# Expert queries computed from the unnormalised input, and the first expert choice made alone

## What is computed

```python
h2 = rms_norm(x, norm2_g) * (1.0 + scale2) + shift2
q = (h2 @ w_query).reshape(T, 8, 256)
s1 = einsum('thd,nd->thn', q[..., :128], sub_keys1)
s2 = einsum('thd,nd->thn', q[..., 128:], sub_keys2)
v1, i1 = top_k(s1, 16); v2, i2 = top_k(s2, 16)
top_s, top_p = top_k(v1[..., :, None] + v2[..., None, :], 16)
e_idx = i1[top_p // 16] * 128 + i2[top_p % 16]
gate = softmax(top_s)
act = gelu(einsum('cd,ced->ce', h2, expert_u[e_idx]))
x = x + gate2 * einsum('ce,ced->cd', gate * act, expert_v[e_idx])
```

## Time and profile before

| | us |
|---|---|
| median of three runs | 2176.35 |
| the three runs | 2176.57, 2171.0, 2176.35 |
| the profiled execution | 2177.08 |
| its span, first to last instruction | 2175.2 |
| PE busy, share of span | 1868.7, 86% |
| DVE busy | 1485.5, 68% |
| ScalarE (ACT) busy | 1016.9, 47% |
| POOL busy | 437.7, 20% |
| mean granted TensorE clock | 0.940 |
| retrieval stage, first gather issued | 433.14 |
| last gather issued | 1074.2 |

### The profile page before, as it was taken

How to read it: one execution, slowest core, us unless ns; L and a number is a source line. 1 busy time by engine, 2 the same in 40 slices (tenths; PEclk the granted TensorE clock), 3 DMA queues, 4 the chain that set the end, 5 groups by cost and what they waited for, 6 DMA issues and landing times. The chain is left out here.

```text
span 2175.2 us, 33251 instructions
## 1 busy us (share of the span) xinstructions
PE 1868.7 (86%) x12082; PEld 1393.0 (64%) x12082; DVE 1485.5 (68%) x2609; ACT 1016.9 (47%) x2046; POOL 437.7 (20%) x457
## 2 busy tenths in 40 slices
PE   4974897878888778777799989889999999779998
PEld 4842887644432222222279988678998988668997
DVE  6675554777767667666466675766677787676666
ACT  2444212445544444444355554467665545335554
POOL 0010220045454434434200000002231330210000
PEclk8987998889999999999999999699999999889999
DMA  8861001399999999999955655035555655224553
GB/s 327 292 219 34 3 3 41 109 406 420 419 419 420 419 420 419 420 420 420 386 185 184 192 172 202 1 116 176 191 181 177 192 175 174 93 84 160 186 189 98
DMA packets 104385, 497.31 MB, mean 229 GB/s; under 512 B 11856, under 2 KB 17232, under 8 KB 71376
## 3 DMA queue, kind: packets, MB, share of 16 engines
q1 hardware_dynamic: 66064, 225.41, 31.2%
q0 software_dynamic: 36864, 268.45, 29.8%
q10 hardware_dynamic: 1344, 1.96, 0.3%
HBM read 494.73 MB, written 1.05 MB: 228 GB/s over the span
## 5 line engine op out<-in xcount | busy, mean ns | idle before, releaser
L247 PE MATMUL ps<-srcs,wh 128*128 128x512 f32 x2064 | 743.2, 402 | 32.1 <-DVE srcs L261 20.4
L1874 PE MATMUL ps<-row,diag 128*128 128x512 f32 x1024 | 502.3, 626 | 121.4 <-ACT diag L1957 121.2
L249 PE MATMUL ps<-srcs,wl 128*128 128x256 f32 x2064 | 583.5, 283 | 0.0
L229 DVE TENSOR_TENSOR wl<-ring,wh 128x1024 fp32r<-128x1024 f32 x362 | 452.3, 1252 | 123.0 <-ACT wh L223 121.8
L247 PEld LDWEIGHTS ps<-srcs,wh 128*128 128x128 f32 x2064 | 392.5, 190 | 127.7 <-issue 35.9
L1874 PEld LDWEIGHTS ps<-row,diag 128*128 128x128 f32 x1024 | 184.0, 195 | 430.1 <-ACT diag L1957 271.7
L2050 DVE CUSTOM_DVE_ANT_0 row<-row,h_tok 128x1024 f32<-128x1024 f32 x256 | 313.8, 1226 | 198.6 <-DMA row<-in_peer_uv,experts 190.7
L223 ACT ACTIVATE wh<-ring 128x1024 fp32r<-128x1024 f32 x362 | 379.1, 1052 | 66.3 <-PE ps L249 43.5
L249 PEld LDWEIGHTS ps<-srcs,wl 128*128 128x128 f32 x2064 | 396.3, 192 | 2.0 <-issue 1.9
L1811 POOL DMA_INDIRECT row<-in_peer_uv,experts x256 | 281.5, 1100 | 393.1 <-PE ps L1874 342.9
L1950 ACT ACTIVATE acts<-dots 128x1 f32<-128x1 f32 x256 | 51.8, 202 | 329.4 <-DVE dots L2050 328.9
(11 more groups left out here) (503 smaller groups left out, 2083.0 us busy)
## 6 DMA issues: line engine op xcount, KB each, us to landing
ring<-in_stream SPq DMA_DIRECT2D x378, 512.0 KB, 3.7
alpha<-in_ada_late SPq DMA_DIRECT2D x12, 512.0 KB, 5.1
beta<-in_ada_late SPq DMA_DIRECT2D x10, 512.0 KB, 6.0
kappa<-in_ada_late SPq DMA_DIRECT2D x10, 512.0 KB, 5.9
row<-in_peer_uv,experts POOLq DMA_INDIRECT x256, 15.4
bias<-in_attn_bias SPq DMA_DIRECT2D x8, 256.0 KB, 5.0
w<-in_cmp_w SPq DMA_DIRECT2D x1, 2048.0 KB, 7.5
xT<-in_xT SPq DMA_DIRECT2D x1, 1024.0 KB, 15.9
```

The costliest lines, as they stand in the source:

```text
L229: nc.vector.tensor_tensor(wl[:, n % PAIRS, :], ring[:, tile % RING, :], wh[:, n % PAIRS, :].bitcast(F32), ALU.subtract).then_inc(tiles_fre ...
L247: nc.tensor.matmul(out, wh[:, n, cols], source.rearrange("p a t -> p (a t)"), start=start, stop=stop, skip_group_check=True)
L249: return nc.tensor.matmul(out[:, 0:S], wl[:, n, cols], source[:, 0, :], start=False, stop=stop, skip_group_check=True)
L1874: last = nc.tensor.matmul(y_part(t, half), diag[:, s % DIAGS, :], row[:, s % ROWS, D + half * 512:D + (half + 1) * 512], start=(slot == 0) ...
```

## The change

The query projection of (x g r + b) is split by linearity, where g is the gain, r the token's inverse root and b the shift.

For the first four query tiles (`UNSHIFTED` = 4) the matmuls take x g alone, split straight from `xT`, so they need neither the root nor the shift. The shift's part is a constant for each query channel: `constants()` multiplies the tile by `shifts` (b in two parts, two columns), 16 narrow matmuls for each tile. The evacuation `out(i)` then takes three DVE instructions: a reduce of the two columns, the sum of both product parts, and plus the constant times the *root* (not its inverse). What comes out is the query times the root. ScalarE multiplies the scores by the inverse root of the token when it copies them (`rstd_tok`, found by turning the root on PE and a reciprocal on 128x2). Tile 3 has its constants after its products, the others ahead of them.

`hT` becomes x g plus b times the root (eight ScalarE instructions, eight DVE instructions), again with the inverse applied on ScalarE's copy to `h_tok`. From it a *second split* (`second_high`, `second_low`) is made for tiles 4 to 15, after the first choice.

The sum of squares is cut (`sums_only`): six of the eight blocks are summed at the end of the projection, and the last two on PE at the start of the retrieval stage (`sum_squares`). `take_rstd` and the root are gone from the projection.

The order changes too. `choose(0)` has nothing among its steps. After it come tiles 2 and 3, `hT`, the gates of head 0, and the second low parts. `choose(1)` moves into the slots of head 0, ahead of `choose(2)`, with a dot before every fourth step in this head (every second in the others). Query tiles 4 and 5 come before the slots on PE, tiles 6 and 7 and scores 2 and 3 among the slots of head 0; from head 1 on, the tiles of head h + 3 lie among the slots of head h. `gate_exp(1)` stands at slot 8, and `finish_gates(1)` after slot 10.

The core of the diff (twelve blanks of indentation removed; the new names of semaphores and buffers, and `project`'s parameter, left out):

```diff
tile(i)
-        if stats:
+        if sums_only:
+            sum_squares(pe, squared, 0, KT - 2)
+        elif stats:
             mean_square(pe, squared, summed)
...
 first = take(T_QUERY)
-EARLY = 4
+EARLY, UNSHIFTED = 2, 4
+def ahead_of(head):
+    return head + 3 if head else NH
...
     return ps[:, 6 + h % 2, :]
+def const_columns(i):
+    return score_bank(min(i, 1))[:, i % 2 * 2:i % 2 * 2 + 2]
+root_bank = ps[:, 3, 0:S]
...
     def query(i):
+        n = split_no(first + i) % PAIRS
         pe.wait_ge(tiles_freed, first + i + 1)
...
             pe.wait_ge(query_out, i - 1)
+        def constants():
+            if i == 0:
+                pe.wait_ge(shift_low, 1)
+            if i % 2 and i > 1:
+                pe.wait_ge(const_out, i)
+            for k in range(KT):
+                cols = slice(k * P, (k + 1) * P)
+                nc.tensor.matmul(const_columns(i), wh[:, n, cols], shifts[:, k, :], start=(k == 0),
+                                 stop=False, skip_group_check=True)
+                last = nc.tensor.matmul(const_columns(i), wl[:, n, cols], shifts[:, k, :], start=False,
+                                        stop=(k == KT - 1), skip_group_check=True)
+            return last
+        if i < UNSHIFTED - 1:
+            constants()
         for k in range(KT):
...
                 pe.wait_ge(src_low, k + 1)
+            if i == UNSHIFTED:
+                pe.wait_ge(second_low, k + 1)
             last = product_both(query_bank(i), first + i, k, srcs[:, k], k == 0, k == KT - 1)
+        if i == UNSHIFTED - 1:
+            last = constants()
         last.then_inc(tiles_used, 1)
...
+    sum_squares(pe, None, KT - 2, KT).then_inc(summed, 1)
     query(0)
+    pe.wait_ge(root, 1)
+    for t in range(TT):
+        last = nc.tensor.transpose(root_bank[:, t * P:(t + 1) * P], rstd[:, t * P:(t + 1) * P], mat("ident"))
+    last.then_inc(root_turned, 1)
     query(1)
...
     score(0)
+    query(2)
+    query(3)
+    score(1)
     turn_h()
-    for h in range(1, EARLY):
-        query(2 * h)
-        query(2 * h + 1)
-        if h >= 2:
-            score(h - 1)
-    score(EARLY - 1)
+    query(4)
+    query(5)
...
         last.then_inc(v_used, 1)
-        ahead = s // TOPK + EARLY
+        ahead = ahead_of(s // TOPK)
+        if s == 1:
+            score(2)
+        if s == 4:
+            query(6)
+        if s == 8:
+            query(7)
+        if s == 13:
+            score(3)
         if ahead < NH:
...
             nc.scalar.activation(scores[t][:, :, h, :], score_bank(h)[:, 2 * t * NE:2 * (t + 1) * NE]
-                                 .rearrange("p (s n) -> p s n", s=2), ACT.Copy).then_inc(score_copied, 1)
+                                 .rearrange("p (s n) -> p s n", s=2), ACT.Copy,
+                                 scale=rstd_tok[:, t:t + 1]).then_inc(score_copied, 1)
...
+    nc.scalar.activation(shifts[:, :, 0], mod[:, 24:32], ACT.Copy).then_inc(shift_high, 1)
+    for k in range(KT):
+        nc.scalar.activation(srch[:, k, :], xT[:, k, :], ACT.Copy, scale=gs[:, 1, k:k + 1]
+                             ).then_inc(src_high, 1)
+    act.wait_ge(scaled, 1)
+    nc.scalar.activation(rstd[:, :], rstd[:, :], ACT.Sqrt).then_inc(root, 1)
+    weight_and_copy(0)
+    weight_and_copy(1)
+    high(act, first + AHEAD + 2)
+    act.wait_ge(inverted, 1)
+    copy_scores(0)
+    for k in range(KT):
+        nc.scalar.activation(hT[:, k, :], rstd[:, :], ACT.Copy, scale=mod[:, 24 + k:25 + k]
+                             ).then_inc(shifted, 1)
+    copy_low(2)
+    weight_and_copy(3)
+    gate_exp(0)
+    copy_scores(1)
+    act.wait_ge(tiles_used, split_no(first + UNSHIFTED - 1) + 1)
     for k in range(KT):
         act.wait_ge(normed, k + 1)
-        nc.scalar.activation(srch[:, k, :], hT[:, k, :], ACT.Copy).then_inc(src_high, 1)
-    weight_and_copy(0)
-    weight_and_copy(1)
-    copy_scores(0)
+        nc.scalar.activation(srch[:, k, :], hT[:, k, :], ACT.Copy).then_inc(second_high, 1)
     for t in range(TT):
...
         nc.scalar.activation(h_tok[:, t, :], ps[:, 2 * t:2 * t + 2, :].rearrange("p b n -> p (b n)"),
-                             ACT.Copy).then_inc(h_copied, 1)
-    for h in range(1, EARLY):
-        weight_and_copy(2 * h)
-        weight_and_copy(2 * h + 1)
-        if h >= 2:
-            copy_scores(h - 1)
-    copy_scores(EARLY - 1)
-    for head in range(LOOKAHEAD):
-        gate_exp(head)
+                             ACT.Copy, scale=rstd_tok[:, t:t + 1]).then_inc(h_copied, 1)
+    weight_and_copy(4)
+    weight_and_copy(5)
     for s in range(TT * SLOTS):
...
             act.wait_ge(gates_done, head + 1)
+        if s == 8:
+            gate_exp(1)
         act.wait_ge(dotted, s + 1)
...
                              ).then_inc(diag_ready, 1)
-        ahead = s // TOPK + EARLY
+        ahead = ahead_of(s // TOPK)
+        if s == 3:
+            copy_scores(2)
+        if s == 7:
+            weight_and_copy(6)
+        if s == 11:
+            weight_and_copy(7)
+        if s == 15:
+            copy_scores(3)
         if ahead < NH:
...
         dve.wait_ge(src_high, k + 1)
-        nc.vector.tensor_tensor(srcl[:, k, :], hT[:, k, :], srch[:, k, :].bitcast(F32), ALU.subtract
-                                ).then_inc(src_low, 1)
+        nc.vector.scalar_tensor_tensor(srcl[:, k, :], xT[:, k, :], gs[:, 1, k:k + 1],
+                                       srch[:, k, :].bitcast(F32), ALU.mult, ALU.subtract
+                                       ).then_inc(src_low, 1)
...
         dve.wait_ge(low_copied, i + 1)
-        if i >= 4:
+        if i >= UNSHIFTED:
             dve.wait_ge(scored, i // 2 - 1)
-        nc.vector.tensor_tensor(queries[:, i % 4, :], query_bank(i)[:, 0:S], low_part[:, i % 2, :], ALU.add
-                                ).then_inc(query_out, 1)
-    for k in range(KT + 2):
-        if k < KT:
-            nc.vector.scalar_tensor_tensor(hT[:, k, :], xT[:, k, :], gs[:, 1, k:k + 1], rstd[:, :],
-                                           ALU.mult, ALU.mult).then_inc(shifting, 1)
-            dve.wait_ge(shifting, k + 1)
-            nc.vector.tensor_scalar(hT[:, k, :], hT[:, k, :], mod[:, 24 + k:25 + k], None, ALU.add
-                                    ).then_inc(normed, 1)
-        if k >= 2:
-            low_of(k - 2)
+            nc.vector.tensor_tensor(queries[:, i % 4, :], query_bank(i)[:, 0:S], low_part[:, i % 2, :], ALU.add
+                                    ).then_inc(query_out, 1)
+            return
+        nc.vector.tensor_reduce(const[:, i % 2:i % 2 + 1], const_columns(i), AXX, ALU.add
+                                ).then_inc(const_out, 1)
+        nc.vector.tensor_tensor(whole[:, i % 2, :], query_bank(i)[:, 0:S], low_part[:, i % 2, :], ALU.add
+                                ).then_inc(whole_out, 1)
+        dve.wait_ge(const_out, i + 1)
+        dve.wait_ge(whole_out, i + 1)
+        dve.wait_ge(root, 1)
+        nc.vector.scalar_tensor_tensor(queries[:, i % 4, :], rstd[:, :], const[:, i % 2:i % 2 + 1],
+                                       whole[:, i % 2, :], ALU.mult, ALU.add).then_inc(query_out, 1)
+    dve.wait_ge(shift_high, 1)
+    nc.vector.tensor_tensor(shifts[:, :, 1], mod[:, 24:32], shifts[:, :, 0].bitcast(F32), ALU.subtract
+                            ).then_inc(shift_low, 1)
+    for k in range(KT):
+        low_of(k)
+        if k == 3:
+            dve.wait_ge(summed, 1)
+            nc.vector.tensor_scalar(rstd[:, :], ps[:, 7, 0:S], 1.0 / D, NORM_EPS, ALU.mult, ALU.add
+                                    ).then_inc(scaled, 1)
     weight(0)
...
     weight(1)
+    dve.wait_ge(root_turned, 1)
+    nc.vector.reciprocal(rstd_tok[:, :], root_bank.rearrange("p (t n) -> p t n", t=TT)[:, :, 0]
+                         ).then_inc(inverted, 1)
     out(1)
+    weight(2)
     dve.wait_ge(counted, 1)
-    early = counter()
-    def early_tile():
-        if early() % 4 == 0:
-            at = early.now // 4 + 3
-            if at < 4 * EARLY:
-                (out if at % 2 else weight)(at // 2)
-    for head in range(LOOKAHEAD):
-        choose(head, early_tile)
-    while early.now // 4 + 3 < 4 * EARLY:
-        early_tile()
-    for head in range(LOOKAHEAD):
-        finish_gates(head)
+    choose(0, lambda: None)
+    out(2)
+    weight(3)
+    out(3)
+    for k in range(KT):
+        dve.wait_ge(shifted, k + 1)
+        nc.vector.scalar_tensor_tensor(hT[:, k, :], xT[:, k, :], gs[:, 1, k:k + 1], hT[:, k, :],
+                                       ALU.mult, ALU.add).then_inc(normed, 1)
+    finish_gates(0)
+    for k in range(KT):
+        dve.wait_ge(second_high, k + 1)
+        nc.vector.tensor_tensor(srcl[:, k, :], hT[:, k, :], srch[:, k, :].bitcast(F32), ALU.subtract
+                                ).then_inc(second_low, 1)
     for head in range(HEADS):
...
                 finish_gates(head + 1)
+            if slot.now == 10 and head == 0:
+                finish_gates(1)
```

(25 more changed lines are left out.)

17 lines of the change are left out of this document (13 added, 4 removed).

## The result

| | before | after |
|---|---|---|
| median, runs taken side by side | 2171.0 (5 runs, 2168.66 to 2176.57) | 2157.62 (5 runs, 2153.72 to 2158.31) |
| ratio, 95% interval | | 0.9924 (0.9911 to 0.9938) |
| the profiled execution, its span | 2177.08, 2175.2 | 2153.96, 2152.2 |
| first gather issued | 433.14 | 415.62 |
| last gather issued | 1074.2 | 1057.05 |

The kernel became 13.4 us faster by the medians; the ratio stands for 16.5 us (13.5 to 19.3). One of the seven runs of a later experiment (the old order with a busy PE) was slow, 3087.02 us at a mean granted clock of 0.553, and is left out of its numbers.

The account below looks back on a forecast made before the run. Gather transfers were taken to bound the retrieval stage, a queue starting with the first gather. First gather -13.0, loads +2.5, first-filling loss -1.0 gave -11.5 us, from the 2176.35 median to 2165.0 (chance 0.5); range 2160.5 to 2171.0.

Parts of the forecast that it names:

- Part 1: Start of the retrieval stage: begins at 396.9 against 400.45, tile 1 done at 407.7, query 1 evacuated at 409.5.
- part 2: First choice without cover: takes 8.2 us, `experts` at 419.8, first gather at 420.1, 13.0 us earlier.
- Rival (c): Narrow matmuls for the constants cost almost nothing: up to 3 us less, 2162; chance 0.1.
- (e): No effect: something unseen, such as a wait for a weight tile, holds the first choice to its old time; chance 0.05.
- Part 3: Behind the first gather: seven ring loads instead of five cost 2.5 us, and 1.0 us of lost transfer time is won.
- 2.5 back: Loads behind the first gather: seven of 512 KB instead of five, each 1.25 us of DMA, costing 2.5 us.
- the lull: DMA stretch from 460 to 470 us at 374 GB/s, 1.1 us short; 1.0 us of it was counted as won.
- The margin: Head 0: gather 8 goes out 20.5 us after `experts`, the queue is dry at 25.2, leaving 4.7 us.
- PE two more: Slot 0 on PE: two us from diag 0, at 18.3 us after `experts`, towards gather 8 at 20.5.
- rival (b): Head 0 is too much for DVE: the DMA loses some 3 to 5 us, 2168 to 2170; chance 0.1.
- Rival (a): PE's clock falls during the narrow runs at the stage's start: 2 to 4 us lost, 2167.0 to 2169.0; chance 0.2.
- Rival (d): PE stays at 1.2 GHz until dot 0: 18 to 19 us lost against 11.5 won, 2183; chance 0.05.

## Why the prediction was wrong

**What bounds the stage** was right: a queue that starts with the first gather. Delaying the first gather by 4.0 delayed the last dot by 4.5.

**Part 1 and part 2** were right, step by step. After the mark: the stage's start at 29.1 (PE's first row), forecast 29.2 (396.9 - 367.71); tile 1's last product at 39.6 (403.32 in the trace of after), forecast 40.0; query 1 evacuated at 41.1, forecast 41.8; `experts` and the first gather at 51.6 and 51.9, forecast 52.1 and 52.4. The gain at the first gather was 13.5 on two profiles each, forecast 13.0. The narrow matmuls stood 0.112 apart, against the 0.115 taken from the earlier trace rows. The 25 ns that the Trainium skill ("TensorE: Matmul & The Clock Gate", section "Wait — 56ns, not 53.3ns?") gives as a floor would have made each run 0.4; this trace has 1.89, so the row decided rightly. Rival (c) is out, and so is (e): nothing held the choice back. Leaving both runs out won only 2 us, less than their length, since they hide the wait for the sources.

**Part 3** has a term that was mis-sized: "2.5 back", less "1.0 won", 1.5 in all. The number of loads was right, and so was the lull: 411 and, in the second profile, 418 GB/s for 374. Yet first gather to last dot grew by 0.4 (mean of two profiles each). I priced a load by its bytes at the full rate, as if the queue were never short of gathers in the first heads; it was. At the 0.6 measured by cutting them, two loads are 1.2, and the lull can't be taken off again, since the loads fill it. What remains between 1.2 and 0.4 these runs can't tell from scatter: two profiles of one kernel differ by up to 0.6 here.

**The margin** of the ninth gather was smaller than forecast, 23.6 us after `experts` instead of 20.5, so 1.6 of 4.7 were left. Two steps were short. ScalarE copies query tile 5 ahead of its steps for slot 0, and PE had tile 5 only 17.1 after `experts` (its clock was at 0.50 from 418 to 428), so slot 0's products could begin at 19.9 and not at 18.3. And the "PE two more" took 3.8, again below full clock. It cost little here; rival (b) stayed away. An 11 us delay was paid at 9.5, so the cover is 1 to 2 us.

**Rival (a)** had the right mechanism and the wrong place. The clock fell in the third narrow run, beside the choice. With runs doubled it fell on the path and cost 9.2 - 3.7 = 5.5 us. Its price, a fall of 3 to 5 us, had no row behind it; the two low stretches of that kernel lasted about 3 and 6.5 us. Rival (d) is the same thing carried on, and did not happen.

**The step that failed is the first line of the sum**: "The profiled execution took 2177.08 (span 2175.2), 0.7 above the median of the three, 2176.35." I took the level of three runs, two of them within 0.25 us of each other, as the kernel's, and built the range from costs alone. Later sessions have medians of 2171.0, 2172.27, 2172.78 and 2172.26 for the same kernel, with single runs from 2164.57 to 2178.77. From 2171.0, the forecast's own -11.5 gives 2159.5, and from 2172.3 it gives 2160.8; 2157.6 was measured. Moved down with the level, the same range would begin at 2155.2 or 2156.5 and hold the result. The miss of 7.4 is thus 5.3 of level (4.1 by the later sessions), 1.6 of the sum (0.5 at the first gather, 1.1 behind it), and a remainder of 0.5 to 1.7 that these runs can't tell from scatter. One of the three runs shown had stood at 2171.0 and said how wide the level is.

What makes the level differ is open. In the two profiles of before the difference lies outside the changed stretch, 6.8 us in code common to all kernels here. No run looked for its cause.

## What to carry to other kernels

Where a stage is a queue of transfers, price a change by the moment of the first one: it passes through whole, while work moved behind it is free until the transfers already under way run out, and small extra transfers cost less than their bytes as long as the queue has gaps. A step that needs another engine's result does not belong among the steps of the chain that starts the queue. Anchor a sum of a few tenths of a per cent on as many runs as are shown, and put their spread into the range beside the costs.

## What the runs showed of the hardware

- TensorE's granted clock falls without any idleness if the work is narrow: behind 32 matmuls of two columns in a row, with PE busy in every microsecond of 396 to 404, it went from 1.00 to 0.51 (402 to 404), though wide products had begun. With 16 between wide ones at full pace it stayed at 1.00, twice. In a third place, where 1.67 us of idleness and eight 128x128 matmuls stood ahead of the 16, it fell to 0.50.
- The same code in two executions had 0.50 and 0.59 of the clock. Matmuls into an unused bank kept it at 1.00.
- A matmul with two columns takes a slot of 0.112 us with its own 128x128 weights. The wide matmuls' weight loads hide, these don't.
- Seven loads of 512 KB issued within 88 us of the first gather cost 4.0 us together beside the gathers, half of what their bytes take at 419 GB/s.
